# One decoder step on one core: two instruction blocks instead of four, with loads and splits moved across the seams

## The chip, the cores and the metric

The kernel runs on one core of one Trainium2 chip. The metric is the device time of one execution in microseconds (us). A core has TensorE (PE in the rows), which multiplies matrices, VectorE (DVE), ScalarE (ACT), GpSimd (POOL) and the queue engine SyncE (SP), which issues most DMAs. Each engine works through its own list of instructions in order, and they meet at semaphores.

## The reference

One step of a hybrid decoder layer, for a prompt of 1024 tokens (with 16 meta tokens ahead of it) and for 8 running sequences of 8 new tokens each, with 4096 cached positions per sequence:

```
xn = rms_norm(x, g_attn);  proj = xn @ w_in             # pool channels, q latent, kv latent, k rope, gates
q  = rms_norm(rope(rms_norm(q_lat) @ w_uq));  k = rms_norm([c_kv @ w_uk, k_rope])
prompt:  o = softmax(q k^T * SCALE, causal) @ (c_kv @ w_uv)
samples: ctx = softmax(q K^T * SCALE) @ c_all;  o = ctx @ w_uv   # c_all: the pages of the cache and the new rows
h  = x + (sigmoid(g1) * pool_mixer(u) + sigmoid(g2) * o) @ w_o
y  = h + relu(rms_norm(h) @ w_ff1)**2 @ w_ff2
```

All is float32. The products that need full precision are made of three passes over a high and a low part (`three_pass`): a number x is split into `hi`, a rounded copy (ScalarE), and `lo = x - hi` (VectorE or GpSimd).

## The kernel before, in words

The program has four stages, each in a block of its own. A block ends for all engines together: its DMAs have landed, semaphores are cleared, the engines meet at a barrier, and only then does the first instruction of the next block start.

1. `front` (to about 414 us). First the latents, queries and keys per tile of 128 tokens; then 20 chunks of 128 columns of `w_in` for the pool channels and the gates. For chunk c, SyncE loads `raw` (L242), ScalarE makes `wh` (L382), VectorE `wl` (L486), TensorE runs `project(c)` (L777) and, between the projections, the small `pooled` products (L787). ScalarE takes the sigmoid of the result (L405), VectorE scales the pooled part (L679), and GpSimd stores each pair of gate chunks to DRAM (`gated`, L282). Behind the last chunk load SyncE writes the states (L244 to L248).
2. `prompt_attention` (422 to 646 us). Its work is a list of items, each a block of values or a block of probabilities, in phases: phase -1 makes the values of the first pair of heads (9 items), and phases 0 to 15 belong to the units (head h, half qc of the queries; unit u is head u // 2). While the items of phase u run, the four score tiles of unit u + 1 are made (`score`, L104 to L106, L1167), every second item where a phase has 9 items or more, else every item. Each score tile goes through VectorE (maximum, L1135), ScalarE (`Exp`, L1084), VectorE (reciprocal) and GpSimd (scaling, L1001) before TensorE turns it (L1211) in the next phase. Phases of even u with h below 6 hold values too (9 or 10 items); phases 12 and 14 have 5 items. Queries and keys of a head are split in one phase: high by ScalarE (L1058), low by GpSimd (L984), at the items that `qk_split_at` names. For head 0 they, and the values' first weights, are loaded and split at the stage's start (L1008 to L1012, L1058, L1062, L1101, L1105).
3. `sample_attention` (649 to 1255 us). 64 groups of 4 cache pages. The last sequence is handled apart: two halves of its context (`first`, `second`: L1727, L1729) are made in banks 2 and 3, and VectorE joins them (L1783 to L1790).
4. `tail` (from 1256 us). TensorE turns the samples' contexts (L2099), multiplies them by `w_uv` (L2106), then runs the output projection `product(half, k, n)` over 8 chunks k of the mixed rows (`mh`, `ml`) and `w_o` (`woh`, `wol`); then the MLP in a loop of 16 passes over three groups of tiles. The last group holds tiles 6, 7 and 8, where tile 8 is the samples' 64 rows, of which a second half is folded in at the very end (L2212). Loads of the mixed rows (L1876), of `w_o` (L1879) and of `w_uv` (L1881) all start with the block.

Of the kernel before, what the change touches and what calls it, by code (L numbers as in the profile page):

```python
# [25 lines left out]
P = 128  # L26
# [8 lines left out]
H = 8  # L35
# [73 lines left out]
def f32(ap):  # L109
    return ap.bitcast(F32)  # L110
# [13 lines left out]
def front(nc, A, C, ps, tiles, xh, xl, cTh, cTl, Q, G, y):  # L124
# [14 lines left out]
    with ExitStack() as ctx:  # L139
        sb, sem = stage_allocator(nc, ctx)  # L140
# [44 lines left out]
        gain_in, table_in, gq_in, pages_in = sem("fr_gain_in"), sem("fr_table_in"), sem("fr_gq_in"), sem("fr_pages_in")  # L185
# [10 lines left out]
        kept = [sem(f"m_kept{i}") for i in range(2)]  # L196
        M = {k: sem("m_" + k) for k in ("wh", "wl", "proj", "up", "uc", "prevp", "prevc", "pool_d", "chain", "sig",
                                        "poolp", "gp", "tailp", "tailc", "tailo")}
        block = ctx.enter_context(nc.Block())
# [50 lines left out]

        @block.gpsimd
        def _(pool):
# [30 lines left out]
            for i in range(2):  # L283
                pool.wait_ge(kept[i], 16 * KD // 2)
# [6 lines left out]
        def _(act):  # L291
# [171 lines left out]
            for c in range(2, NCH):  # L463
                if c < 4:
                    copy_channels(c)
                else:
                    sigmoid(c)
                if c + 2 < NCH:
                    split_chunk(c + 2)

        @block.vector
        def _(dve):
# [196 lines left out]
            for j in range(KD):  # L669
                if 6 + 2 * j < NCH:  # L670
                    split_chunk(6 + 2 * j)
                for b, (lo, hi) in enumerate(groups):
                    i = 3 * j + b

                    if b == 2 and 7 + 2 * j < NCH:
# [5 lines left out]
                                                   op0=ALU.mult, op1=ALU.mult).then_inc(M["gp"], 1)  # L681

# [174 lines left out]
def prompt_attention(nc, A, C, ps, cTh, cTl, Q, G, m, B, arrived, c_rows):  # L857
# [41 lines left out]
    for u in range(-1, len(units)):  # L899
        todo = phase_items(u)  # L900
        phase_start[u] = len(items)
        apart = 2 if len(todo) >= 9 else 1
        for n, item in enumerate(todo):
            items.append(item)
            scored = u + 1 < len(units) and n % apart == 0 and n // apart < NT
            tile_at.append(NT * (u + 1) + n // apart if scored else None)
# [5 lines left out]
    qk_split_at = {phase_start[2 * h] + 1 + 2 * k: (h + 1, k) for h in range(H - 1) for k in range(2)}  # L912
    w_split_at = {phase_start[4 * (p - 1) - 1] + 7: p for p in range(1, H // 2)}
# [12 lines left out]
    with ExitStack() as ctx:  # L926
        sb, sem = stage_allocator(nc, ctx)
        w_raw = sb("pa_w_raw", [P, 2, 2 * VH])
        w_h, w_l = sb("pa_w_h", [P, 2, 2, 2 * VH], F32R), sb("pa_w_l", [P, 2, 2, 2 * VH], F32R)
        qh, ql = sb("pa_qh", [QK, 2, SEQ], F32R), sb("pa_ql", [QK, 2, SEQ], F32R)  # L930
        kh, kl = sb("pa_kh", [QK, 2, TP], F32R), sb("pa_kl", [QK, 2, TP], F32R)
        vh, vl = sb("pa_vh", [P, 2, NK, 2 * VH], F32R), sb("pa_vl", [P, 2, NK, 2 * VH], F32R)
        prob = [(sb("pa_prob0", [P, sum(wide[:NT])]), range(NT)), (sb("pa_prob1", [P, sum(wide[NT:])]), range(NT, 2 * NT))]
        raw = [sb("pa_q_raw", [QK, SEQ]), sb("pa_k_raw", [QK, TP])]
        gm, mixed = sb("pa_gm", [P, 2, 2, QC]), sb("pa_mixed", [P, 2, QC])
        ph, pl = sb("pa_ph", [P, 4, QC], F32R), sb("pa_pl", [P, 4, QC], F32R)
        late = sb("pa_late", [P, P])
        late_r, ident_r = sb("pa_late_r", [P, P], F32R), sb("pa_ident_r", [P, P], F32R)
        ntop, den, rden = sb("pa_ntop", [P, NT]), sb("pa_den", [P, NT]), sb("pa_rden", [P, NT])
        w_in, g_in, raw_in = sem("pa_w_in"), [sem(f"pa_g_in{i}") for i in range(2)], [sem("pa_q_in"), sem("pa_k_in")]  # L940
        m_out = [sem(f"pa_m_out{i}") for i in range(2)]
        S = {k: sem("pa_" + k) for k in ("late0", "late", "const", "w_hi", "w_lo", "qk_hi", "k_lo", "q_lo", "scores", "max",
                                         "exp", "rden", "scaled", "t", "hi", "lo", "pv", "out", "m")}
        block = ctx.enter_context(nc.Block())
        flat = ps[:].rearrange("p b n -> p (b n)")
        sources = ((raw[0][:], qh, ql), (raw[1][:], kh, kl))
# [33 lines left out]
        def _(pool):  # L980
            def low(h, k):
                src, hi, lo = sources[k]
                pool.wait_ge(S["qk_hi"], 2 * h + k + 1)
                nc.gpsimd.tensor_tensor(lo[:, h % 2, :], src, f32(hi[:, h % 2, :]),  # L984
                                        ALU.subtract).then_inc(S["k_lo" if k else "q_lo"], 1)

            nc.gpsimd.memset(B["c_new"][:, 0:KV], 0.0).then_inc(arrived["zeros"], 1)
            nc.gpsimd.memset(B["c_new"][:, KV:KV + 1], 1.0)
            nc.gpsimd.memset(late[:], 0.0).then_inc(S["late0"], 1)
            pool.wait_ge(S["late0"], 1)  # L990
            nc.gpsimd.affine_select(out=late[:], in_=late[:], compare_op=ALU.is_ge, fill=NEG, base=0,
                                    pattern=[[1, P]], channel_multiplier=-1).then_inc(S["late"], 1)
            low(0, 0)
            for n in range(N):
                if n in qk_split_at:
                    low(*qk_split_at[n])
# [8 lines left out]
        def _(sp):  # L1005
            def load_values(p):
                cols = A["w_uv"].rearrange("(k p) h d -> p k (h d)", p=P)[:, :, 2 * VH * p:2 * VH * (p + 1)]
                sp.dma_start(w_raw[:], cols).then_inc(w_in, 16)  # L1008

            def load_head(h):  # L1010
# [1283 lines left out]
```

## Time and profile before

| | us |
|---|---|
| median of 3 runs (lowest, highest) | 2149.71 (2149.37, 2150.7) |
| the profiled execution's own time | 2148.84 |
| its span, first to last instruction | 2146.9 |
| TensorE busy in it | 2069.8 (96%) |
| VectorE, ScalarE, GpSimd busy | 1177.6, 814.9, 384.4 |
| mean granted TensorE clock, share of full speed | 0.984 |

TensorE leaves 77.1 us of the span idle. The granted clock has two levels, full (2.4 GHz, shown as 1.00) and half (1.2 GHz, shown as 0.50). A row of the timeline reads: start in us, duration in us, engine, line, operation, output <- inputs, shape, count, and in brackets how long the engine had been idle and what released it. "SPq" is SyncE's DMA queue.

### The profile page before, as it was taken

To read this page: it belongs to the slowest core of one execution; us is meant where nothing else is said; L and a number is where in the kernel's file an instruction comes from. 1 tells how busy PE (TensorE), PEld (TensorE's weight loads), DVE (VectorE), ACT (ScalarE), POOL (GpSimd) and SP (SyncE) were. 2 spreads that over 40 slices of the span, in tenths; PEclk is the share of its full clock that TensorE was granted. 3 is DMA by queue.
4 is the path that set the end of the run, shared out by engine and by line. 5 is a ranking of instruction groups with operands and counts; after the bars stand their busy time and mean duration, and the time that the engine had idled before them with its cause. 6 is when DMAs were issued, how large, how long until landed. Compare 5 with 4: busy or idle time off the path is not lost. (4 is left out here: it accounts for less than half of the span.)

```text
span 2146.9 us, 35239 instructions
## 1 busy us (share of the span) xinstructions
PE 2069.8 (96%) x12669; PEld 1909.3 (89%) x12669; DVE 1177.6 (55%) x2356; ACT 814.9 (38%) x1589; POOL 384.4 (18%) x441
## 2 busy tenths in 40 slices
PE   7999999799988999999999989999999999999998
PEld 6889999688878999999999968889999899998997
DVE  5773311167756777767776743554444444445444
ACT  5552111166644566656665632321111122111121
POOL 2110000044421155535553510000000000000000
PEclk9999999899998999999999989999999999999999
DMA  4332222235313222222222062111111111111102
GB/s 169 92 105 71 61 82 87 92 89 165 107 50 83 57 56 67 62 73 65 66 64 73 15 213 86 46 53 41 57 39 39 39 39 59 39 54 44 39 20 89
DMA packets 146190, 152.69 MB, mean 71 GB/s; under 512 B 50694, under 2 KB 122102, under 8 KB 145021
## 3 DMA queue, kind: packets, MB, share of 16 engines
q1 hardware_dynamic: 140325, 128.28, 20.4%
q0 software_dynamic: 5728, 22.65, 3.3%
q8 instruction: 77, 1.26, 0.3%
q14 instruction: 60, 0.49, 0.1%
HBM read 124.77 MB, written 25.97 MB: 70 GB/s over the span
## 5 line engine op out<-in xcount | busy, mean ns | idle before, releaser
L104 PE MATMUL ps<-mh,f_w1h 128*128 128x384 f32 (+1 forms) x768 | 250.6, 326 | 0.0
L106 PE MATMUL ps<-mh,f_w1l 128*128 128x384 f32 (+1 forms) x768 | 250.5, 326 | 0.0
L105 PE MATMUL ps<-ml,f_w1h 128*128 128x384 f32 (+1 forms) x768 | 250.3, 326 | 0.0
L2042 ACT ACTIVATE tail_room<-ps 128x384 f32<-128x384 f32 (+1 forms) x96 | 45.5, 474 | 502.1 <-PE ps L106 502.1
L1495 ACT ACTIVATE sq<-ps 128x512 f32<-128x512 f32 x256 | 153.0, 598 | 208.9 <-PE ps L106 208.8
L2087 DVE TENSOR_TENSOR t_m<-t_m,ps 128x512 f32<-128x512 f32 x256 | 171.7, 685 | 107.0 <-PE ps L106 107.0
L105 PE MATMUL ps<-f_late_l,f_late_h 128*128 128x512 f32 x512 | 199.9, 390 | 0.0
L106 PE MATMUL ps<-f_late_h,f_late_l 128*128 128x512 f32 x512 | 199.8, 390 | 0.0
L104 PE MATMUL ps<-f_late_h 128*128 128x512 f32 x512 | 199.3, 389 | 0.0
L2067 DVE TENSOR_TENSOR tail_room<-tail_room 128x384 f32<-128x384 f32 (+1 forms) x96 | 51.5, 536 | 253.7 <-ACT tail_room L2042 253.7
L104 PE MATMUL ps<-wq,cTh 128*128 128x320 f32 x512 | 172.0, 336 | 2.3 <-DVE g_attn_b L1575 1.5
L1577 DVE TENSOR_REDUCE ss<-sq 128x8 f32<-128x512 f32 x256 | 172.9, 675 | 0.0
L106 PE MATMUL ps<-wq,cTl 128*128 128x320 f32 x512 | 158.2, 309 | 0.0
L105 PE MATMUL ps<-wq,cTh 128*128 128x320 f32 x512 | 157.8, 308 | 0.0
L104 PEld LDWEIGHTS ps<-mh,f_w1h 128*128 128x128 f32 x768 | 144.2, 188 | 1.9
L105 PEld LDWEIGHTS ps<-ml,f_w1h 128*128 128x128 f32 x768 | 144.2, 188 | 1.8
L106 PEld LDWEIGHTS ps<-mh,f_w1l 128*128 128x128 f32 x768 | 144.1, 188 | 0.0
L106 PE MATMUL ps<-w_late,cTl 128*128 128x256 f32 x512 | 143.3, 280 | 0.0
L104 PE MATMUL ps<-w_late,cTh 128*128 128x256 f32 x512 | 143.0, 279 | 0.0
L105 PE MATMUL ps<-w_late,cTh 128*128 128x256 f32 x512 | 143.0, 279 | 0.0
L1575 DVE TENSOR_TENSOR g_attn_b<-ps,g_attn_b 128x64 f32<-128x64 f32 x256 | 56.8, 222 | 151.7 <-ACT sq L1495 150.3
L106 PEld LDWEIGHTS ps<-f_late_h,f_late_l 128*128 128x128 f32 x512 | 96.1, 188 | 20.2
(348 smaller groups left out, 5029.9 us busy)
## 6 DMA issues: line engine op xcount, KB each, us to landing
f_raw<-in_w_ff SPq DMA_DIRECT2D x32, 1024.0 KB, 5.3
c_ring<-in_cache_kv_latent SPq DMA_DIRECT2D x192, 128.0 KB, 2.0
m_raw<-in_w_in SPq DMA_DIRECT2D x20, 512.0 KB, 4.0
gated<-gate POOLq DMA_DIRECT2D x8, 1088.0 KB, 4.7
pa_gm<-gated SPq DMA_DIRECT2D x16, 512.0 KB, 4.6
c_early<-in_cache_kv_latent SPq DMA_DIRECT2D x64, 128.0 KB, 2.1
fr_x<-in_x_prompt SPq DMA_DIRECT2D x8, 512.0 KB, 3.6
mixed<-pa_mixed SPq DMA_DIRECT2D x16, 256.0 KB, 2.1
```

The source lines that it names most:

```text
L104: nc.tensor.matmul(out, lh, rh, start=first, stop=False)
L105: nc.tensor.matmul(out, lh, rl, start=False, stop=False)
L106: return nc.tensor.matmul(out, ll, rh, start=False, stop=last)
L1495: nc.scalar.activation(sq[:, j % 2, :].rearrange("p (a n) -> p a n", a=2), ps[:, kn_bank(j):kn_bank(j) + 2, 0:HALF], ACT.Square).then_inc( ...
L1575: nc.vector.tensor_tensor(summed[:, p1, j * HQ:(j + 1) * HQ], ps[:, kn_bank(j), HALF:HALF + HQ], rope[:, p1, j * HQ:(j + 1) * HQ], ALU.add ...
L1577: nc.vector.tensor_reduce(ss[:, p1, j * H:(j + 1) * H], sq[:, j % 2, :].rearrange("p (h d) -> p h d", d=NOPE), AX.X, ALU.add).then_inc(S[" ...
L2042: nc.scalar.activation(z[:, a, 0:w], ps[:, 2 * par + a, 0:w], ACT.Relu).then_inc(S["relu"], 1)
L2067: nc.vector.tensor_tensor(z[:, a, 0:w], z[:, a, 0:w], z[:, a, 0:w], ALU.mult).then_inc(S["z"], 1)
L2087: nc.vector.tensor_tensor(part, part, ps[:, bank, :], ALU.add).then_inc(S["y"], 1)
```

## The change

- `front` and `prompt_attention` share one block, `sample_attention` and `tail` another. At both merged seams the engines no longer meet, and explicit waits stand for what has to be over.
- The prompt's tiles are laid out ahead of the front (`prompt_tiles`), so that those of head 0 lie on room that is free before the front ends. SyncE loads head 0's queries, keys and value weights behind the state writes, ScalarE splits them after chunk 15, VectorE and GpSimd make the low parts after step j = 5 of the last loop.
- Phase -1 starts with a value item and scores at items 1, 3, 5, 7 (before 0, 2, 4, 6). Later weights are split at item 4 of their phase, not 7. Head 7 is split in phase 11, not 12.
- SyncE issues the loads of `w_uv`, of three chunks of `w_o` and of four chunks of mixed rows while the samples end; ScalarE and VectorE split the first two or three before `second` is over. TensorE puts output products ahead of and between the turning of the contexts and their product with `w_uv`.
- In the MLP the pieces of the last group go in the order tile 8, 6, 7; the fold stands before the last addition, and the last tile's two halves are stored one by one.

```diff
@@ front, sync
             sp.wait_ge(M["tailo"], 16 * (2 + NSEQ))
+            sp.wait_ge(M["pool_d"], 8)
+            for done in qk_out:
+                sp.wait_ge(done, 16 * N)
+            load_head(nc, Q, T, E, 0)
+            load_values(nc, A, T, E, 0)
@@ front, gpsimd: for j in range(KD)
                 pool.dma_start(G[j], gate[:, j % 2]).then_inc(kept[j % 2], 16)
-            for i in range(2):
-                pool.wait_ge(kept[i], 16 * KD // 2)
+                if j == KD - 3:
...
+                    pool.wait_ge(E["qk_hi"], 1)
+                    nc.gpsimd.tensor_tensor(T["ql0"][:], T["raw_q"][:], f32(T["qh0"][:]), ALU.subtract).then_inc(E["q_lo"], 1)
@@ front, scalar: for c in range(2, NCH), after split_chunk(c + 2)
+                if c == NCH - 5:
+                    act.wait_ge(E["w_in"], 16)
+                    nc.scalar.activation(T["w_h0"][:], T["w_raw"][:], ACT.Copy).then_inc(E["w_hi"], 1)
+                    act.wait_ge(E["raw_in"][0], 16)
+                    nc.scalar.activation(T["qh0"][:], T["raw_q"][:], ACT.Copy).then_inc(E["qk_hi"], 1)
+                    act.wait_ge(E["raw_in"][1], 16)
+                    nc.scalar.activation(T["kh0"][:], T["raw_k"][:], ACT.Copy).then_inc(E["qk_hi"], 1)
@@ front, vector: for j in range(KD)
+                if j == KD - 3:
+                    dve.wait_ge(E["w_hi"], 1)
+                    nc.vector.tensor_tensor(T["w_l0"][:], T["w_raw"][:], f32(T["w_h0"][:]), ALU.subtract).then_inc(E["w_lo"], 1)
+                    dve.wait_ge(E["qk_hi"], 2)
+                    nc.vector.tensor_tensor(T["kl0"][:], T["raw_k"][:], f32(T["kh0"][:]), ALU.subtract).then_inc(E["k_lo"], 1)
@@ prompt_attention
+        first = 1 if u < 0 else 0
...
-    qk_split_at = {phase_start[2 * h] + 1 + 2 * k: (h + 1, k) for h in range(H - 1) for k in range(2)}
-    w_split_at = {phase_start[4 * (p - 1) - 1] + 7: p for p in range(1, H // 2)}
+    qk_split_at = {phase_start[2 * h] + 1 + 2 * k: (h + 1, k) for h in range(H - 2) for k in range(2)}
+    qk_split_at.update({phase_start[2 * (H - 2) - 1] + 3 + 2 * k: (H - 1, k) for k in range(2)})
+    w_split_at = {phase_start[4 * (p - 1) - 1] + 4: p for p in range(1, H // 2)}
@@ prompt_attention, tensor
+                if s == 0:
+                    pe.wait_ge(S["mask"], 2)
+                if s == 1:
+                    pe.wait_ge(E["gp"], 3 * H)
...
-            pe.wait_ge(S["const"], SEQ // P - 1 + 2)
+            pe.wait_ge(E["sig"], 2 * H)
@@ tail, sync
+            sp.wait_ge(SA["ctx"], NG - 12)
+            sp.dma_start(raw2[:], A["w_uv"].rearrange("(k p) h d -> p k (h d)", p=P)).then_inc(uv_in, 16)
+            sp.wait_ge(SA["rope"], NG)
+            for i in range(3):
+                load_o(i)
+            sp.wait_ge(SA["ctx"], NG - GS)
+            for k in range(4):
+                load_m(k)
...
@@ tail, tensor
+            pe.wait_ge(SA["gmax"], NSEQ + 1)
+            pe.wait_ge(SA["summed"], GP * NG)
+            pe.wait_ge(SA["sq"], GP * NG)
+            pe.wait_ge(SA["scaled_first"], 1)
+            head(0, (0, 1, 2, 4))
+            pe.wait_ge(SA["ctxn"], NSEQ)
             for rc in range(2):
                 for b in range(NSEQ):
                     last = nc.tensor.transpose(...)
                 last.then_inc(S["ctx_turned"], 1)
+            head(0, (3,))
+            head(1, range(5))
             pe.wait_ge(uv_in, 16)
...
+            for k in range(2):
+                head(k, (5, 6))
+            pe.wait_ge(S["gated"], 1)
+            for k in range(2):
+                head(k, (7,))
+            for k in range(2, KD):
+                head(k, range(NT - 1))
@@ tail
-    pieces = [[(t, hf) for t in g for hf in range(2)] for _c, g in groups]
+    pieces = [[(t, hf) for t in g for hf in range(2)] for g in ((0, 1, 2), (3, 4, 5), (8, 6, 7))]
@@ tail, vector: dve_step, after the addition of piece i
+                    if i == 4 and not valid(2):
+                        dve.wait_ge(folded_in, 16)
+                        dve.wait_ge(S["y"], 6 * (NS - 1) + 2)
+                        nc.vector.tensor_tensor(h8[0:TS, :], h8[0:TS, :], halves, ALU.add).then_inc(folded, 1)
```

`head(k, ns)` waits for `wol` and `ml` of chunk k and runs `product(0, k, n)` for the n named. The last stores now go: `halves` once tile 8 is added (y at 2 of the last 6), tile 6, the first half of tile 7, the samples' rows after the fold, the second half of tile 7.

## Rows read from the trace of the kernel before

**Rows 1.** Waits of TensorE, whole span: who for whom, us in total, times, longest.
```profile
PE ps L104 <- DVE pa_kl L1101: 17.0, 1, 17.0
PE ps L104 <- issue: 6.7, 1, 6.7
PE ps L2106 <- DMA f_raw<-in_w_uv: 6.6, 1, 6.6
...
PE ps L1707 <- PEq L926: 4.6, 1, 4.6
```
**Rows 2.** Windows: stretch, length, busy by engine (instructions), TensorE clock, DMA share, GB/s.
```profile
431.00:434.20 3.20, 3.20 (x15) 3.20 (x16) 1.17 (x2) 0.01 (x1) 0.00 (x0) 0.50 0.27 86
607.59:611.40 3.81, 3.81 (x17) 3.60 (x17) 1.22 (x2) 1.14 (x3) 0.69 (x1) 0.50 0.02 4
1270.70:1273.90 3.20, 3.20 (x10) 2.52 (x10) 2.85 (x4) 2.78 (x4) 0.02 (x1) 0.50 1.03 399
```
**Rows 3.** Timeline of TensorE across the first seam, to the first turned probabilities.
```profile
412.60 1.37 PE L787 MATMUL ps<-dT,wpm 128*128 128x368 f32 x4
...
431.00 0.56 PE L104 MATMUL ps<-pa_kh,pa_qh 96*128 96x264 f32 x1 [17.03 <-DVE pa_kl L1101]
...
443.67 0.66 PE L1211 MATMUL ps<-ident,pa_prob 128*128 128x128 f32 x4
```
**Rows 4.** Timeline of the other engines across the first seam, one engine after another.
```profile
413.49 1.18 DVE L679 SCALAR_TENSOR_TENSOR gate<-ps,pscale,gate 128x368 f32<-128x368 f32 x2 [11.95 <-PE ps L787]
...
428.75 2.11 DVE L1101 TENSOR_TENSOR pa_kl<-pa_k_raw,pa_kh 96x1040 fp32r<-96x1040 f32 x1 [5.07 <-ACT pa_kh L1058]
...
412.80 1.20 ACT L405 ACTIVATE gate<-ps 128x368 f32<-128x368 f32 x3 [11.94 <-PE ps L777]
...
427.38 2.38 POOL L984 TENSOR_TENSOR pa_ql<-pa_q_raw,pa_qh 96x1024 fp32r<-96x1024 f32 x1 [3.97 <-ACT pa_qh L1058]
```
**Rows 5.** DMA issues of 350 to 432 us: count, KB each, median us to landing.
```profile
pa_k_raw<-k_rows SPq DMA_DIRECT2D x1, 390.0 KB, 4.8
```
**Rows 6.** Timeline of SyncE, ScalarE and VectorE in the front's last loop.
```profile
366.61 2.67 SPq L248 DMA_DIRECT2D out_state_s<-tail  x8
...
373.98 1.20 ACT L405 ACTIVATE gate<-ps 128x368 f32<-128x368 f32 x3 [10.40 <-PE ps L777]
...
387.12 1.20 ACT L405 ACTIVATE gate<-ps 128x368 f32<-128x368 f32 x3 [10.99 <-PE ps L777]
...
376.16 1.23 DVE L486 TENSOR_TENSOR m_wl<-m_raw,m_wh 128x1024 fp32r<-128x1024 f32 x1 [0.93 <-ACT m_wh L382]
```
**Rows 7.** Timeline of GpSimd in phase 12 of the prompt's attention.
```profile
605.12 2.37 POOL L984 TENSOR_TENSOR pa_kl<-pa_k_raw,pa_kh 96x1040 fp32r<-96x1040 f32 x1 [1.48 <-ACT pa_kh L1058]
```
**Rows 8.** Timeline of TensorE: start of phase 13, start of phase 15.
```profile
607.59 0.56 PE L104 MATMUL ps<-pa_kh,pa_qh 96*128 96x264 f32 x1 [6.70 <-issue]
...
632.49 1.09 PE L1211 MATMUL ps<-ident,pa_prob 128*128 128x128 f32 x4 [2.84 <-POOL pa_prob L1001]
```
**Rows 9.** Timeline of TensorE, then ScalarE, across the seam of samples and tail.
```profile
1244.60 0.64 PE L1385 MATMUL ps<-ch,prob_hl 128*128 128x258 f32 x4
...
1253.20 0.59 PE L1729 MATMUL ps<-c_new,prob 128*64 128x257 f32 x2
1255.95 1.30 PE L2099 MATMUL ps<-ident,room 64*128 64x64 f32 x16 [2.15 <-PEq L1319]
1263.89 7.09 PE L2106 MATMUL ps<-h,f_raw 128*128 128x64 f32 x32 [6.64 <-DMA f_raw<-in_w_uv]
...
1259.51 1.06 ACT L2145 ACTIVATE mh<-t_m 128x1024 fp32r<-128x1024 f32 x1 [1.63 <-DMA t_m<-mixed]
```
**Rows 10.** Timeline of VectorE, then SyncE, at the end of the kernel.
```profile
2137.37 0.69 DVE L2087 TENSOR_TENSOR h<-h,ps 128x512 f32<-128x512 f32 x1 [0.23 <-PE ps L2015]
2141.50 1.22 DVE L2212 TENSOR_TENSOR h<-h,f_raw 64x1024 f32<-64x1024 f32 x1 [3.44 <-DMA f_raw<-h]
...
2142.74 0.54 SPq L1905 DMA_DIRECT2D out_y_s<-h  x1
```

More of the change, by code:

```diff
@@ L121, in gate_chunks, with prompt_tiles, sb, load_head @@
     return cols
-def front(nc, A, C, ps, tiles, xh, xl, cTh, cTl, Q, G, y):
+def prompt_tiles(nc):
+    T = {}
+    with ExitStack() as ctx:
+        def sb(name, shape, dt=F32):
+            T[name] = ctx.enter_context(nc.sbuf_tensor("pa_" + name, list(shape), dt))
+        NK = TP // P + 1
+        wide = [min(P * (t + 2), TP) for t in range(SEQ // P)]
+        for name in ("vh", "vl"):
+            sb(name, [P, 2, NK, 2 * VH], F32R)
+        for name, n in (("qh1", SEQ), ("ql1", SEQ), ("kh1", TP), ("kl1", TP)):
+            sb(name, [QK, n], F32R)
+        for name in ("w_h1", "w_l1"):
+            sb(name, [P, 2, 2 * VH], F32R)
+        sb("prob0", [P, sum(wide[:4])])
+        sb("prob1", [P, sum(wide[4:])])
+        sb("mixed", [P, 2, 512])
+        sb("gm", [P, 2, 2, 512])
+        sb("room", [P, 80])
+        for name, n in (("qh0", SEQ), ("ql0", SEQ), ("kh0", TP), ("kl0", TP)):
+            sb(name, [QK, n], F32R)
+        sb("raw_k", [QK, TP])
+        sb("late", [P, P])
+        for name in ("ntop", "den", "rden"):
+            sb(name, [P, 4])
+        sb("room1", [P, 68])
+        for name in ("ph", "pl"):
+            sb(name, [P, 4, 512], F32R)
+        sb("ident_r", [P, P], F32R)
+        sb("late_r", [P, P], F32R)
+        sb("raw_q", [QK, SEQ])
+        sb("w_raw", [P, 2, 2 * VH])
+        for name in ("w_h0", "w_l0"):
+            sb(name, [P, 2, 2 * VH], F32R)
+    return T
+def load_head(nc, Q, T, E, h):
+    nc.sync.dma_start(T["raw_q"][:], Q[0][:, h, TS + META:TS + TP]).then_inc(E["raw_in"][0], 16)
+    nc.sync.dma_start(T["raw_k"][:], Q[1][:, h, TS:TS + TP]).then_inc(E["raw_in"][1], 16)
+def load_values(nc, A, T, E, p):
+    cols = A["w_uv"].rearrange("(k p) h d -> p k (h d)", p=P)[:, :, 2 * VH * p:2 * VH * (p + 1)]
+    nc.sync.dma_start(T["w_raw"][:], cols).then_inc(E["w_in"], 16)
+def front(nc, A, C, ps, tiles, xh, xl, cTh, cTl, Q, G, y, block, T, E):
     N = len(tiles)
@@ L195, in front @@
         prev_in, map_in = sem("m_prev_in"), sem("m_map_in")
[L196 to L199, printed above, removed]
+        M = {k: sem("m_" + k) for k in ("wh", "wl", "proj", "uc", "prevp", "prevc", "pool_d", "chain",
+                                        "poolp", "tailp", "tailc", "tailo")}
+        M["sig"], M["gp"], kept, pages_in = E["sig"], E["gp"], E["kept"], E["pages_in"]
         w_all = A["w_in"].rearrange("(k p) n -> p k n", p=P)
@@ L926, in prompt_attention @@
     with ExitStack() as ctx:
[L927 to L940, printed above, removed]
+        _sb, sem = allocator(nc, ctx)
@@ new lines, in prompt_attention @@
+        two = lambda name: [T[name + "0"][:], T[name + "1"][:]]
+        w_h, w_l, qh, ql, kh, kl = (two(name) for name in ("w_h", "w_l", "qh", "ql", "kh", "kl"))
+        vh, vl, gm, mixed, ph, pl, late, late_r, ident_r, ntop, den, rden, w_raw = (
+            T[name] for name in ("vh", "vl", "gm", "mixed", "ph", "pl", "late", "late_r", "ident_r", "ntop", "den", "rden", "w_raw"))
+        prob = [(T["prob0"], range(NT)), (T["prob1"], range(NT, 2 * NT))]
+        w_in, raw_in = E["w_in"], E["raw_in"]
@@ L941, in prompt_attention @@
+        g_in = [sem(f"pa_g_in{i}") for i in range(2)]
         m_out = [sem(f"pa_m_out{i}") for i in range(2)]
-        S = {k: sem("pa_" + k) for k in ("late0", "late", "const", "w_hi", "w_lo", "qk_hi", "k_lo", "q_lo", "scores", "max",
-                                         "exp", "rden", "scaled", "t", "hi", "lo", "pv", "out", "m")}
-        block = ctx.enter_context(nc.Block())
+        S = {k: sem("pa_" + k) for k in ("mask", "padded", "scores", "max", "exp", "rden", "scaled", "t", "hi", "lo", "pv", "out", "m")}
@@ L1806, in _, with tail @@
             steps(pool_step)(pool)
-def tail(nc, A, C, ps, room, ctxs, m_rows, G, x_tiles, results):
+        return S
+def tail(nc, A, C, ps, room, B, m_rows, G, x_tiles, results, block, SA):
     NF = FF // FB
```

262 lines of the change are left out of this document (145 added, 117 removed).

## The prediction

> **What bounds the kernel now.** TensorE is busy 2069.8 of 2146.9 us on the page. So I read first who kept it waiting, over the whole span [rows 1]. The reader is to see that a few single waits make most of the idle time, and each has a place: 17.0 us for head 0's low part of the keys (the seam front to prompt), 6.7 us labelled "issue" inside the prompt's attention, 6.6 us for a load of `w_uv` behind the seam samples to tail, and 4.6 us at the seam prompt to samples. Then the windows around these places [rows 2]: TensorE's clock stands at 0.50 for over 3 us behind each of three gaps, so each also costs half of that stretch. Then the timelines of all engines at each place [rows 3 to 10], to see what is late next. Through the MLP loop (1300 to 2137 us) TensorE waits for nothing; the change can win only at the seams, in the prompt's phases and at the end.
>
> **First seam.** TensorE's last front product ends at 412.60 + 1.37 = 413.97; it starts again at 431.00, and the first turned probabilities stand at 443.67 [rows 3]: 29.7 us. The work between 431.00 and 443.67 takes 12.67 us, of which 3.20 at half clock [rows 2], so 12.67 - 1.6 = 11.07 at full clock. The change lets it follow at once. What is late next:
> - the last sigmoid, which frees the banks, ends at 412.80 + 1.20 = 414.0 [rows 4]: nothing to speak of;
> - the first score waits for the mask's copies, which VectorE makes behind its last scaling, at 413.49 + 1.18 = 414.67 [rows 4]. With one value item ahead of it, that is 0.25 us;
> - the chain maximum, `Exp`, reciprocal, scaling. It now starts one item later, and the weights' split stands in it at item 4. By the same durations it ends about when TensorE wants it; I take 0.3 us, bounds 0 and 3 (the whole wait of 2.84 us that phase 15 has for the same chain [rows 8]).
>
> New length about 11.07 + 0.6 = 11.7, gain 29.7 - 11.7 = 18.0 us, between 15 and 18.6.
>
> **What the moved loads and splits cost in the front.** SyncE's state writes are issued until 366.61 + 2.67 = 369.3 [rows 6]; with some 2 to 3 us until they have landed, the three loads go out at about 372, and the slowest kind lands 4.8 us after issue [rows 5]: about 377. ScalarE, which by then stands at its wait behind chunk 15, makes three high parts (some 2.7 us) until 380. Queued behind them are its sigmoid of 373.98 and the split of chunk 18, now done by about 382; VectorE waits with them, makes the two low parts, and its low part of chunk 18, which stood at 376.16, ends at about 383.5. TensorE needs it when chunk 17 is through, which ended before the sigmoid at 387.12 [rows 6]. So 3.5 us are to spare, and the splits cost nothing: project(17) hides them. GpSimd waits there too, but its next store is not due before step 6 is over. If that cover were gone, each us beyond is a us; bounds 0 and 5 us. VectorE's low part of the keys took 2.11 us beside GpSimd's low part of the queries, and ended 1.1 us after it [rows 4], as if it had done nothing before. The Trainium skill ("SBUF — State Buffer", section "Who interferes with whom") has the rule: a VectorE instruction with both inputs in SBUF is shut out while a GpSimd instruction reads SBUF. By that rule the pair takes up to 1.1 us more in its new place too, and VectorE's later subtractions can be held there; my margin shrinks to 2.4 us and stays a margin, and the sum stays as it is.
>
> **Head 7's split.** The 6.7 us are no issue time. TensorE starts at 607.59 with the first score of head 7 [rows 8], and that needs the low part of its keys, which GpSimd ended at 605.12 + 2.37 = 607.49 [rows 7]. Phase 12 has 5 items with a score at each, so two GpSimd instructions of 2.4 us do not fit between its four scalings. After the change they lie in phase 11. The gap goes (6.7), and so does the half clock behind it, 3.81 us [rows 2], worth 1.9: together 8.6. What is late next is the scaling of the last tile: phase 14 has the same shape without a split, and there TensorE waits 2.84 us for it [rows 8]. In phase 13 the first score of head 7 (1.5 us at half clock, about 1.0 at full) covers part: 1.5 to 1.8 stay. In phase 11 the two low parts push the last scaling behind the time at which phase 12 starts, by about 1 us; it has 9 items, but no values to fill it. So 8.6 - 1.7 - 1.4 = 5.5 us, between 2.5 (phase 12's gap comes back in phase 11 with a clock dip) and 7.5.
>
> **Seam prompt to samples.** It stays a block's end; its 4.6 us [rows 1] and the samples' preparation at half clock stay. 0, between -1 and 1 (more semaphores are cleared there).
>
> **Seam samples to tail.** The last product of `second` ends at 1253.20 + 0.59 = 1253.79 [rows 9]. Before: 2.15 idle, 1.30 turning the contexts, 6.64 idle, 7.09 for `w_uv` at half clock, then output products with 3.20 us at half clock [rows 2, 9], to 1273.9: 20.1 us. The same work at full clock is 1.30 + 7.09 / 2 + 1.6 = 6.45. Is all else ready? The mixed rows are loaded from the 56th context group on, which ends at 1244.60 + 0.64 = 1245.24 [rows 9]. In the old seam the first of them reached ScalarE at 1259.51 [rows 9], 3.6 us after the block's start at 1255.9; the same puts it at 1248.9, `mh` at 1250, `ml` (1.2 us) at 1251.2 and chunk 1 a little over 1 us later, at 1252.5. TensorE is then in `second` until 1253.79, so both are there. The join of the contexts (three small VectorE instructions) has four output products, about 2.8 us, beside it, ScalarE's copies have six (4 us), and `w_uv` was loaded long before. DMA is nearly idle from 1200 to 1255, so the loads collide with nothing. Gain 20.1 - 6.45 = 13.65; I take 13.6. If the first chunks came 3 us late and the clock fell, 9; at best 14.5.
>
> **The end.** TensorE ends at 2137.3; the last addition is done at 2137.37 + 0.69 = 2138.06, then `halves` lands (3.44 us idle), the fold takes 1.22, the samples' rows are stored from 2142.74 [rows 10], and the span ends 4.16 us later. After: tile 8 is added about 5 us before TensorE's end, `halves` lands before or around the fourth addition (a 1.5 MB store of tiles 3 to 5 is on the queues then), the fold goes between the fifth and sixth addition, which moves the sixth by some 0.5 to 1 us, to about 2138.8. Its store takes the same 4.16 us: 2143.0, and with the slower landing 2143.6. Gain 3.7, between 2.5 and 4.2.
>
> **Loop.** The other order of the last group changes nothing while each addition (0.69 us) is shorter than TensorE's piece. 0 us.
>
> **The sum.** 18.0 + 5.5 + 13.6 + 3.7 = 40.8 us. Against the profiled execution's 2148.84: 2108.0. The median of the runs, 2149.71, is 0.9 above that execution, so 2109 is my number.
>
> **Rivals.**
> 1. *The front pays* (head 0's loads come too late for ScalarE and VectorE, which hold back chunk 18). For it: SyncE waits until ten small writes have landed, and a 1088 KB store starts at about 376. Against: the 3.5 us of room above. 3 us of stall and a clock dip of 1.6: 2113.6.
> 2. *The tail starts hungry* (mixed rows too late, TensorE stands between `second` and the first output product, and the clock drops). For it: only 8.5 us lie between the 56th group and the end of `second`, and four 512 KB loads start together. Against: an empty queue. 4.6 us: 2113.6.
> 3. *The exponent chain or phase 11 takes back what is won* (TensorE waits for scalings in phase 0 and phase 12). For: the first scores and splits come later in their phases; against: small pieces. 3 us on each of the two terms: 2115.
> 4. *Slower than before.* With tile 8 first, TensorE's two short pieces (4 matmuls for 6) open the group's bank cycle, and VectorE still has the squares and low parts of the next group to do; if each of the 16 passes stalled TensorE, the price would be 16 times the stall. It decides from 40.8 / 16 = 2.6 us a pass; at 3 us, 48 - 40.8 = 7 us slower: 2157. Against: TensorE has no wait in that loop, and VectorE is busy only half of it.
> 5. *It does not do what it says*: if the engines still met at the merged seams (a wait that stands for a barrier, say that of the front's last GpSimd store), only head 7 and the end would win: 2149.7 - 9.2 = 2140.5.
>
> **How the numbers follow.** Forecast 0.74, rivals 1 and 2 0.08 each, 3 0.05, 4 0.03, 5 0.01, others of no effect 0.01. The likeliest gives 2109. All terms at their best are 44.8 + 1 = 45.8, thus 2104; rivals 1 to 3 reach 2115, and two of them together 2119. Range 2104 to 2119. This kernel's measurement tells about 0.2% from no change (4.3 us); faster by more: 0.96, within: 0.01, slower: 0.03.
>
> **What would show it.** Right: at the first seam TensorE's wait for `pa_kl` is gone and its clock stays 1.00 from 410 to 430; no wait at chunk 18; in phase 13 a wait under 2 us for GpSimd instead of 6.7; output products directly behind `second` at full clock; about 5.5 us from TensorE's last product to the end, for 9.55 now; the seam prompt to samples as before. Wrong: a wait of TensorE for `m_wl` near 387, a gap before the first output product, a wait over 3 us at the start of phase 12, or TensorE idle in the MLP loop.

## The result, and the profile after

| | before | after |
|---|---|---|
| median of 4 runs (lowest, highest), us | 2149.64 (2149.37, 2150.7) | 2117.85 (2117.62, 2120.17) |
| ratio, 95% interval | | 0.9855 (0.9843 to 0.9867) |
| the profiled execution's own time, span | 2148.84, 2146.9 | 2120.17, 2118.4 |
| TensorE busy, granted clock | 2069.8, 0.984 | 2072.5, 0.994 |

The gain is 31.8 us, inside the range of the forecast and 9 short of its 40.8. The profiled execution of after is the slowest of its four, so between the two traces the gain is 28.5 us. To see where it lies, I read the same events of TensorE in both timelines; the last column is one of the experiments further down, put beside them here because it answers the question that the first two raise.

| time from the start of the span to, us | before | after | won by then | aligned version, won by then |
|---|---|---|---|---|
| first turned probabilities | 443.67 | 427.42 | 16.25 | 16.90 |
| end of the prompt's attention | 644.42 | 622.38 | 22.04 | 23.11 |
| start of the samples | 649.00 | 627.54 | 21.46 | 22.53 |
| end of `second` | 1253.79 | 1232.29 | 21.50 | 24.07 |
| first product of `w_ff1` | 1377.50 | 1344.35 | 33.15 | 37.55 |
| last product | 2137.34 | 2111.49 | 25.85 | 37.35 |
| end of the span | 2146.9 | 2118.4 | 28.5 | 39.5 |

The line to stop at is the last product: between 1344 and 2111 us, where the forecast had put 0, after gives back 7.3 us. Everything before it went nearly as forecast. First the waits of TensorE in after (who for whom, us in total, times, longest), which answer to [rows 1]:

```profile
PE ps L785 <- DVE fr_xn L604: 8.9, 1, 8.9
PE ps L1284 <- POOL pa_prob L1077: 7.2, 5, 2.9
PE ps L1779 <- PEq L2383: 5.2, 1, 5.2
...
PE ps L104 <- DVE pa_vl L1212: 0.5, 1, 0.5
```

The 17.0, the "issue" of 6.7 and the 6.6 for `w_uv` are gone; the seam prompt to samples stays, at 5.2 us where it was 4.6. None of the waits in the list lies in the MLP. The timeline of TensorE in after at the first seam, in phase 13 and across the seam of samples and tail (start, duration, engine, line, operation), answering to [rows 3, 8, 9]:

```profile
413.46 1.37 PE L868 MATMUL ps<-dT,wpm 128*128 128x368 f32 x4
414.92 0.39 PE L104 MATMUL ps<-pa_w_h,p_cTh 128*128 128x256 f32 x1
...
427.42 0.66 PE L1284 MATMUL ps<-ident,pa_prob 128*128 128x128 f32 x4
...
588.14 0.63 PE L1284 MATMUL ps<-ident,pa_prob 128*128 128x128 f32 x4 [1.89 <-POOL pa_prob L1077]
...
1231.70 0.59 PE L1801 MATMUL ps<-c_new,prob 128*64 128x257 f32 x2
1232.23 0.50 PE L104 MATMUL ps<-f_w1h,mh 128*128 128x512 f32 x1
...
1235.21 1.21 PE L2223 MATMUL ps<-ident,room 64*128 64x64 f32 x16
...
1240.61 3.68 PE L2232 MATMUL ps<-h,f_raw 128*128 128x64 f32 x32
```

The reader is to see three things: the first value product at 414.92 follows the front's last product, which ends at 414.83, with no gap worth the name; the 6.70 us ahead of head 7's score have become 1.89 for a scaling; and the output products follow `second` with no bracket at all, the product with `w_uv` at 3.68 us in place of 7.09. The clock at the two seams (windows of after: stretch, length, busy by engine with the instructions in brackets, TensorE clock, DMA share, GB/s), where [rows 2] had 0.50:

```profile
414.90:430.00 15.10, 14.40 (x101) 12.95 (x101) 10.08 (x31) 8.73 (x23) 2.72 (x5) 1.00 0.33 110
...
1231.70:1236.00 4.30, 4.30 (x27) 3.10 (x26) 2.81 (x6) 0.66 (x2) 1.06 (x2) 1.00 1.14 339
```

Then the front's last loop in after (SyncE's queue, ScalarE, VectorE, GpSimd), answering to [rows 6]. The moved splits are the rows of `pa_`; the "SPq" row is the first of the moved loads. The low part of chunk 18 is `m_wl`, done at 385.1, and the sigmoid behind which TensorE wants it is that of 387.98:

```profile
373.07 0.32 SPq L167 DMA_DIRECT2D pa_raw_q<-q_rows  x1
...
378.81 0.63 ACT L541 ACTIVATE pa_w_h<-pa_w_raw 128x512 fp32r<-128x512 f32 x1 [14.38 <-DMA pa_w_raw<-in_w_uv]
...
380.48 2.43 POOL L352 TENSOR_TENSOR pa_ql<-pa_raw_q,pa_qh 96x1024 fp32r<-96x1024 f32 x1 [2.67 <-ACT pa_qh L543]
381.26 1.17 ACT L473 ACTIVATE gate<-ps 128x368 f32<-128x368 f32 x3
381.38 2.62 DVE L762 TENSOR_TENSOR pa_kl<-pa_raw_k,pa_kh 96x1040 fp32r<-96x1040 f32 x1 [1.22 <-ACT pa_kh L545]
...
383.93 1.21 DVE L562 TENSOR_TENSOR m_wl<-m_raw,m_wh 128x1024 fp32r<-128x1024 f32 x1
...
387.98 1.20 ACT L473 ACTIVATE gate<-ps 128x368 f32<-128x368 f32 x3 [4.60 <-PE ps L858]
```

And the end in after (VectorE and SyncE's queue), answering to [rows 10]: the fold comes first, and the last addition stands behind it.

```profile
2111.45 1.22 DVE L2195 TENSOR_TENSOR h<-h,f_raw 64x1024 f32<-64x1024 f32 x1 [0.64 <-DMA f_raw<-h]
2112.60 0.67 DVE L2191 TENSOR_TENSOR t_m<-t_m,ps 128x512 f32<-128x512 f32 x1
...
2113.30 0.57 SPq L2009 DMA_DIRECT2D out_y_p<-t_m  x1
```

**The 7.3 us of the MLP.** TensorE is never idle there, and runs the same products. So I grouped its products between 1400 and 2090 us, each shape by itself (line, engine, operation, names, shape, count, busy us, mean ns of one, idle us before). Before:

```profile
L106 PE MATMUL ps<-f_late_h,f_late_l 128*128 128x512 f32 x466 | 181.8, 390 | 0.0
L105 PE MATMUL ps<-f_late_l,f_late_h 128*128 128x512 f32 x465 | 181.6, 390 | 0.0
L104 PE MATMUL ps<-f_late_h 128*128 128x512 f32 x465 | 181.0, 389 | 0.0
L104 PE MATMUL ps<-mh,f_w1h 128*128 128x384 f32 x463 | 155.0, 335 | 0.0
...
L106 PE MATMUL ps<-mh,f_w1l 128*128 128x384 f32 x462 | 154.7, 335 | 0.0
```

After:

```profile
L105 PE MATMUL ps<-f_late_l,f_late_h 128*128 128x512 f32 x463 | 183.5, 396 | 0.0
L106 PE MATMUL ps<-f_late_h,f_late_l 128*128 128x512 f32 x463 | 181.8, 393 | 0.0
L104 PE MATMUL ps<-f_late_h 128*128 128x512 f32 x462 | 181.6, 393 | 0.0
L106 PE MATMUL ps<-mh,f_w1l 128*128 128x384 f32 x464 | 156.9, 338 | 0.0
L104 PE MATMUL ps<-mh,f_w1h 128*128 128x384 f32 x464 | 155.8, 336 | 0.0
```

The products of 512 columns (the second matrix, in the tiles `f_late_h` and `f_late_l`) take 3 to 6 ns more. From start to start it is 227.9 ns before and 231.9 after, over the three kinds; with 36 of them in a full group that is 8.19 us before and 8.35 after, and over a pass 0.42 us, 16 passes 6.7 us. Small, but on an engine that is busy without a break there is nothing that hides it. The first matrix (tiles `f_w1h` and `f_w1l`) shows little: its products of 384 columns take 334 or 335 ns before and 335 to 338 after. From start to start the products of the first matrix add up to 371.9 us over the MLP before and 372.4 after, those of the second to 368.5 and 375.0.

Two things differ there: the order of the pieces, which the prediction had weighed, and the places of the tail's tiles. The merged block lets the tail's first tiles fill while the samples still use theirs, so `mh`, `ml`, `f_late_h`, `f_late_l` and h were given other places, and the eighth part of `f_late_l` became a tile of its own. Before, the tail's tiles all start 416 bytes over a multiple of 2048 in their partition; after, `f_late_l` starts at 928 and `f_late_h` at 1536. The traces hold no addresses: such places are added up from the tiles' sizes in the kernels.

### The profile page after: what moved, and what is told of

It is laid out like the page before. It is cut to its first block, busy times and chain, and to the rows that moved or that the text cites. A ratio compares the mean times of both kernels' runs of the same rounds, so it can differ in the third digit from the quotient of the medians.

```text
span 2118.4 us, 35220 instructions
## 1 busy us (share of the span) xinstructions
PE 2072.5 (98%) x12669; PEld 1903.3 (90%) x12669; DVE 1174.0 (55%) x2356; ACT 814.3 (38%) x1589; POOL 384.6 (18%) x441
## 4 chain that ended last, share of the span: by engine, by line
PE 66%; DVE 2%; ACT 1%; issue 1%; DMA 0%; DVEq 0%
PE ps L104 19%; PE ps L106 19%; PE ps L105 19%; PE ps L1498 2%; PE ps L1457 1%; PE ps L1463 1%; PE ps L2118 1%; DVE ss L1649 0%; DVE cTl L1655 0%; ACT sq L1567 0%; PE ps L2072 0%; PE ps L2116 0%; PE ps L2119 0%; DVE var L1725 0%; PE ps L1555 0%
## 5 line engine op out<-in xcount | busy, mean ns | idle before, releaser
L104 PE MATMUL ps<-mh,f_w1h 128*128 128x384 f32 (+1 forms) x768 | 251.0, 327 | 0.0
L104 PE MATMUL ps<-f_late_h 128*128 128x512 f32 x512 | 201.2, 393 | 0.0
L104 PE MATMUL ps<-wq,cTh 128*128 128x320 f32 x512 | 172.0, 336 | 2.4 <-DVE g_attn_b L1647 1.8
L104 PEld LDWEIGHTS ps<-mh,f_w1h 128*128 128x128 f32 x768 | 144.2, 188 | 2.1
L104 PE MATMUL ps<-w_late,cTh 128*128 128x256 f32 x512 | 143.0, 279 | 0.0
L104 PEld LDWEIGHTS ps<-f_late_h 128*128 128x128 f32 x512 | 96.3, 188 | 22.2
```

What stands on the lines that cost most here:

```text
L104: nc.tensor.matmul(out, lh, rh, start=first, stop=False)
```

## Experiments

### The two merged seams, each alone

`s1_first_merge` has the front and the prompt's attention of after, samples and tail of before; `s2_second_merge` the reverse.

> Front and prompt's attention as after (one block, early loads of head 0, head 7 split in phase 11), samples and tail as before. Theory (the terms of the profile of after add up and do not touch each other): the first turned probabilities 17 us earlier counted from the front's end, phases 11 to 13 another 5.8, nothing else: 23 us, so 2127. Rival (the slower pace of the 512-column products in the MLP comes with the block structure): part of it shows here too, products at over 0.230 us and a gain of 16 to 20. Forecast's own terms: 18.0 + 5.5 = 23.5.

> Front and prompt's attention as before, samples and tail as after (one block, other layout of the tail's tiles, last group in the order 8, 6, 7, early fold). Theory: the seam itself gives 13.6, the end 2.7, and the MLP loop gives back 7 us, because its 512-column products take 0.2320 instead of 0.2277 us: 8 to 9 us net, 2141. Rival (the slower pace was a matter of that one execution): products at 0.2277 and 15 to 17 us net, 2133.

Measured: 2127.22 us (ratio 0.9896, 0.988 to 0.9913) and 2141.71 us (0.9963, 0.9948 to 0.9977). The first merge wins 22.8 us of 2149.98, the second 8.3; together 31.1, and both at once 31.8. So as far as these intervals tell (some 3 us either way) they do not help or hinder each other. What each still waits for at seams, from TensorE's waits (for whom, us in total, times, longest). First merge alone:

```profile
PE ps L2179 <- DMA f_raw<-in_w_uv: 6.3, 1, 6.3
...
PE ps L2172 <- PEq L1392: 2.1, 1, 2.1
```

Second merge alone:

```profile
PE ps L104 <- DVE pa_kl L1101: 16.8, 1, 16.8
...
PE ps L104 <- issue: 6.7, 1, 6.7
```

Each loses exactly the waits of its own seam. The MLP, from its first product to its last, takes 759.84 us in the first and 767.14 in the second: the slow products come with the second merge.

### Order of the pieces, or places of the tiles

`o1_order_only` is the kernel before with one line of after, `l1_layout_only` the kernel before with the tail's places of after:

```diff
 o1:
-    pieces = [[(t, hf) for t in g for hf in range(2)] for _c, g in groups]
+    pieces = [[(t, hf) for t in g for hf in range(2)] for g in ((0, 1, 2), (3, 4, 5), (8, 6, 7))]
 l1:
-        mh = sb("mh", [P, KD, TOK], F32R)
-        ml = sb("ml", [P, KD, TOK], F32R)
...
+        _room0 = sb("t_room0", [P, 128])
+        mh = sb("mh", [P, KD, TOK], F32R)
+        late_l = sb("f_late_l", [P, (KD - 1) * 512], F32R)
...
+        m = sb("t_m", [P, H, SEQ])
         late_h = sb("f_late_h", [P, KD * 512], F32R)
-        late_l = sb("f_late_l", [P, KD * 512], F32R)
```

> The kernel before with one edit: the last group's pieces in the order tile 8, 6, 7. Theory A (address): no change of pace, 2149 to 2150, at most 0.5 us at the very end, since the samples' rows are added earlier but stored as before. Theory B (order): 36 products take 8.35 us instead of 8.19 and the time goes up by 6 to 7 us, 2156.

> The kernel before with one edit: the tail's tiles lie at the addresses that they have in the kernel after. Theory A (where the operands lie in SBUF sets the pace of the 512-column products): each takes 0.2315 to 0.2325 us instead of 0.2277 in the MLP, 36 products 8.35 us instead of 8.19, the time goes up by 6 to 9 us, to 2156 to 2159. Theory B (the order of the last group sets it): no change, 2149 to 2150.

Measured: 2149.96 us for the order (1.0001, 0.9992 to 1.0011; MLP 760.04) and 2158.48 us for the places (1.0041, 1.0027 to 1.0055; MLP 767.06). The order is free, as forecast. The places alone, with not one instruction changed, cost 8.5 us (9.5 between the spans): 7.2 in the MLP and some 1.8 in the output projection in front of it. That projection takes 109.35 us from its first product to the MLP's, for 106.76 before, but 4.7 us of it stand at half clock here and 3.2 before, which makes 0.8 of the 2.6. With the clock full throughout, after takes 112.12 us for the same work and the aligned version 110.31: again 1.8.

### Which property of a place

The first five are before or after with nothing but padding tiles put in ([P, 8] is 8 numbers, 32 bytes, per partition); the last gives after's tail another order of tiles. Padding behind a pair keeps the tiles after it where they were. In `p2` this puts `f_late_l` 1856 over a multiple of 2048, not 1024 as its expectation says; the distance is the one it names.

```diff
 p1 (before):  +        _pad0 = sb("t_pad0", [P, 128])     # ahead of late_h; 384 more behind late_l
 p2 (before):  +        _pad0 = sb("t_pad0", [P, 360])     # between late_h and late_l; 152 behind
 d5 (before):  +        _pad0 = sb("t_pad0", [P, 128])     # between late_h and late_l; 384 behind
 d2 (before):  +        _pad = sb("t_pad", [P, 8])         # ahead of all tiles of the tail
 a2 (after):   +        _room1b = sb("t_room1b", [P, 8])   # ahead of ml; room2 8 less
               +        _room3 = sb("t_room3", [P, 8])     # ahead of late_h
 a1 (after):
-        _room0 = sb("t_room0", [P, 128])
+        late_l7 = sb("f_late_l7", [P, 512], F32R)
         mh = sb("mh", [P, KD, TOK], F32R)
         late_l = sb("f_late_l", [P, (KD - 1) * 512], F32R)
...
-        _room2 = sb("t_room2", [P, 608])
+        late_h7 = sb("f_late_h7", [P, 512], F32R)
+        st = sb("f_st", [P, NT, 4])
+        _room2 = sb("t_room2", [P, 244])
...
-        late_h = sb("f_late_h", [P, KD * 512], F32R)
+        _room3 = sb("t_room3", [P, 232])
+        late_h = sb("f_late_h", [P, (KD - 1) * 512], F32R)
```

> The kernel before with 512 bytes of padding ahead of f_late_h and 1536 behind f_late_l: both tiles start 512 bytes further (928 over a multiple of 2048, where everything in the tail stood at 416), their distance from one another stays 0 over a multiple of 2048, and all other tiles stand at 416 as before. Theory A (where a tile starts by itself sets the pace of the products that read it): the 36 products of a second-matrix group go from 8.19 us to about 8.35 and the time from 2150 to 2156 or so. Theory B (what counts is how the two tiles that one product reads lie to each other): late_h and late_l still lie alike, 8.19 us and 2150.

> The kernel before with 1440 bytes of padding between f_late_h and f_late_l (608 behind them): late_l starts 1024 over a multiple of 2048, late_h stays at 416, so their distance over a multiple of 2048 is the one of the kernel after. Theory B (the distance between the two tiles of one product): products that read both, 105 and 106, slow down by some 5 ns each, those of line 104 (late_h alone) do not; a group of 36 takes about 8.3 us and the time is 2153 to 2156. Theory A (each tile's own start): only the products with late_l as moving operand change, if 1024 is a bad place; 2150 to 2153. If neither, 2150.

> The kernel before with 32 bytes of padding ahead of all of the tail's tiles, so that each starts on a multiple of 64, 448 over a multiple of 2048, and their distances stay what they were. Theory B (the distance over 64 between the tiles counts, not the place): as before, 8.19 us a group and 2150. Theory C (a tile on a multiple of 64 is a slow one, one at 32 over is fast): all 512-column products slow down, L104 as well, 8.35 us or more and 2156 to 2161.

> The kernel after with three paddings only: ml (with h8, m8 and f_late_l7 behind it) starts 32 bytes later and so do f_late_h and f_raw2. So all operands of the tail's products start 32 over a multiple of 64, as in the kernel before; over a multiple of 2048 they stand at 416, 928, 1184 and 1568, so not alike. Theory (the runs so far fit it: 512-column products are slow where late_h and late_l lie 32 bytes apart over a multiple of 64, in after, in the layout put into before, in the tiles 1440 bytes apart, and in the version meant to be aligned, where late_h stood at 448 for a rounding; fast where they lie alike): the group of 36 products takes 8.19 to 8.22 us instead of 8.35 and the time is 2109.5 to 2112. Rival (places have to be alike over 2048 bytes or more, or 64 plays no part): 8.33 us or more, 2116 to 2119.

> The kernel before with 512 bytes of padding between f_late_h and f_late_l (1536 behind them): they lie 512 apart over a multiple of 2048, late_h at 416 and late_l at 928. Distances of 32, 608 and 640 over a multiple of 2048 gave 764.7 to 767.1 us for the MLP, 0 gave 759.8 to 760.0. If the pace repeats every 512 bytes (or 256): 759.8 to 760.3 and 2150. If it wants 1024 or the whole 2048 of one operand's row: 764.5 to 766 and 2155 to 2157.

> The kernel after with its tail's tiles moved so that each starts 416 over a multiple of 2048, as in the kernel before (f_late_h and f_late_l keep their first seven parts and have the eighth apart; h also stays in its place, 320 over). If the places of f_late_h, f_late_l, mh and ml are all that slowed the 512-column products, a group of 36 products goes from 8.35 us back to 8.19 and the time from 2117.9 to about 2109.5 to 2111.5. Rival (the pace came from something else that the merged block has, such as another place of h): 2116 to 2118, groups stay at 8.35.

| kernel | late_h against late_l, bytes over a multiple of 2048 (of 512) | second matrix, mean ns from start to start | MLP on TensorE, us | median, us |
|---|---|---|---|---|
| before | 0 (0) | 227.9 | 759.84 | 2149.6 to 2150.2 |
| both tiles 512 further (`p1`) | 0 (0) | 227.9 | 759.84 | 2150.01 |
| all tiles 32 further (`d2`) | 0 (0) | 227.9 | 759.85 | 2149.86 |
| 512 apart (`d5`) | 1536 (0) | 227.9 | 759.84 | 2149.62 |
| 1440 apart (`p2`) | 608 (96) | 231.9 | 765.88 | 2156.97 |
| places of after in before (`l1`) | 608 (96) | 231.8 | 767.06 | 2158.48 |
| after | 608 (96) | 231.9 | 767.14 | 2117.85 |
| after, 32 bytes put in twice (`a2`) | 640 (128) | 231.1 | 764.74 | 2115.9 |
| after, meant to be aligned (`a1`) | 32 (32) | 231.7 | 765.75 | 2117.94 |

Shifting both tiles by 512 bytes, or all by 32, leaves the MLP's time to the hundredth of a us. Changing their distance to 608 makes it longer: `p2`, which changes nothing else of what the MLP reads, has the whole slowdown of the second matrix (368.5 to 374.9 us over the MLP, 375.0 in after). Nor is it the place of one of them: the slow `a1` has `f_late_h` at 448, where it stands in the fast `d2`, and `f_late_l` at 416, where it stands before. The clearest pair is the one with padding between the two tiles, in the groups of 1400 to 2090 us. Padding of 1440 bytes:

```profile
L105 PE MATMUL ps<-f_late_l,f_late_h 128*128 128x512 f32 x469 | 185.9, 396 | 0.0
L104 PE MATMUL ps<-f_late_h 128*128 128x512 f32 x468 | 184.0, 393 | 0.0
L106 PE MATMUL ps<-f_late_h,f_late_l 128*128 128x512 f32 x468 | 183.9, 393 | 0.0
```

Padding of 512 bytes:

```profile
L106 PE MATMUL ps<-f_late_h,f_late_l 128*128 128x512 f32 x467 | 182.3, 390 | 0.0
L105 PE MATMUL ps<-f_late_l,f_late_h 128*128 128x512 f32 x466 | 182.0, 391 | 0.0
L104 PE MATMUL ps<-f_late_h 128*128 128x512 f32 x466 | 181.4, 389 | 0.0
```

My theories fell one by one here. "Each tile's own start" fell with `p1` and `p2`, and the forecast that L104, which reads `f_late_h` alone, stays as it is fell with `p2` (393 ns). "Alike over a multiple of 64" fitted all kernels run by then and was not enough: after with 32 bytes put in has its operands alike over 64 and regains 2.4 us of 7.3 (2115.9, ratio 0.9842, 0.9829 to 0.9856). Of the 2.4 the second matrix, whose products read `f_late_h` and `f_late_l` alone, has 1.3, and keeps 5.2 of its 6.5; the first matrix has most of the rest. That places alike over 64 but not over 512 keep most of the loss rests on this one kernel, which also has `ml` elsewhere than the others. And the first aligned version missed (2117.94 for 2109.5 to 2111.5) for a plain reason: the allocator starts a tile on a multiple of 32 bytes, `f_st` (144 bytes) and the padding behind it (976) are not such multiples, each was rounded up by 16, and `f_late_h` stood at 448, not 416.

### The aligned version

```diff
 against the version that was meant to be aligned:
-        _room3 = sb("t_room3", [P, 232])
+        _room3 = sb("t_room3", [P, 224])
```

> The kernel after with its tail laid out so that w1h, w1l, mh, ml, f_late_h and f_late_l all start 416 over a multiple of 2048 (h stays where it was, at 1568): the version meant to be aligned before, less the 32 bytes that stood in it. Theory D (late_h and late_l must lie a multiple of 2048, or of a power of two between 64 and 2048, apart: 0 gave 759.84 us for the MLP on TensorE in four kernels; 32, 608 and 640 gave 765.8, 765.9 to 767.1, and 764.7): the MLP takes 759.8 to 760.5 us instead of 767.1 and the time is 2109 to 2111. Rival (the distance must be a multiple of 4096 or more, here it is 45 times 2048, or the slowness has to do with h or with the input's raw tiles, which this kernel has in other places): 764 us or more, 2114 to 2118.

Measured: 2109.82 us (2109.2 to 2110.92), ratio to before 0.9815 (0.9801 to 0.9828) where after has 0.9855 (0.9843 to 0.9867), 8.0 us less than after; the MLP takes 760.04 us. It differs from the version that was meant to be aligned by 32 bytes in the place of `f_late_h` and of the raw tile behind it, and by 8.1 us. Of the 9.4 us between the two traces, 6.4 lie where the tiles are read (MLP 765.75 to 760.04, output projection 111.02 to 110.31) and 1.65 in the samples, which go with the clock (end of the next part); the rest lies in the front and the prompt's attention, which are the same in both. It is faster than before and than after. Its groups of 1400 to 2090 us:

```profile
L105 PE MATMUL ps<-f_late_l,f_late_h 128*128 128x512 f32 x468 | 182.6, 390 | 0.0
L104 PE MATMUL ps<-f_late_h 128*128 128x512 f32 x469 | 182.6, 389 | 0.0
L106 PE MATMUL ps<-f_late_h,f_late_l 128*128 128x512 f32 x468 | 182.5, 390 | 0.0
```

### Head 7's split put back

```diff
-    qk_split_at = {phase_start[2 * h] + 1 + 2 * k: (h + 1, k) for h in range(H - 2) for k in range(2)}
-    qk_split_at.update({phase_start[2 * (H - 2) - 1] + 3 + 2 * k: (H - 1, k) for k in range(2)})
+    qk_split_at = {phase_start[2 * h] + 1 + 2 * k: (h + 1, k) for h in range(H - 1) for k in range(2)}
```

> The kernel after with head 7's queries and keys split in phase 12 again (the old position), all else as it is. Theory (the 5.8 us that the phases of the prompt's attention gained are the wait for that split): the wait of TensorE there is back and the time is 2117.9 + 5.8 = about 2123.7, with all of it between the start of phase 12 and the end of the prompt's attention. Rival (the gain came from the other moved pieces, the split of the last values and the late masks): at most 2119.

Measured: 2126.42 us (0.9889, 0.9872 to 0.9905), 8.6 slower than after. The theory holds: the rival had 2119 at most. Its size holds less well. The wait is back, in TensorE's timeline:

```profile
591.56 0.56 PE L104 MATMUL ps<-pa_kh,pa_qh 96*128 96x264 f32 x1 [6.74 <-issue]
```

and the prompt's attention ends at 628.60 instead of 622.38, 6.2 us later; the last product comes 6.4 later. That is what the trace shows of the 8.6. The rest is the 2.3 us by which the profiled execution of after lies above its median: against profile and profile the difference is 2126.55 - 2120.17 = 6.4.

## Why the prediction was right, and by how much it missed

| term | forecast | after | aligned version |
|---|---|---|---|
| first seam, to the first turned probabilities | 18.0 | 16.25 | 16.90 |
| head 7's split and the phases | 5.5 | 5.8 | 6.2 |
| seam prompt to samples | 0 | -0.6 | -0.6 |
| samples | 0 | 0 | 1.5 |
| seam samples to tail, to the MLP | 13.6 | 11.65 | 13.5 |
| MLP | 0 | -7.3 | -0.2 |
| the end | 3.7 | 2.65 | 2.15 |
| sum (between the traces) | 40.8 | 28.5 | 39.5 |

- **The step that failed is the loop's.** The sum had 0 us for it; it gave back 7.3. "The other order of the last group changes nothing" was right (`o1_order_only`: 1.0001). "0 us" for the loop was wrong, because I priced only what the diff does to the order of instructions there and not that it moves the tiles the products read (`l1_layout_only`: 767.06 us for 759.84 with the order of before). It also ate most of what the seam samples to tail lacks: 13.5 in the aligned version against 11.65. That is 7.1 + 1.85 = 9 us of the 12.3 that are missing between the traces.
- **First seam.** The mechanism was as told: no wait for `pa_kl`, clock at 1.00, first scores after the masks, one short wait of 0.46 us for a low part of the values. From the front's last product it is 29.70 before, 12.59 after: 17.1 won. The 12.59 are 0.9 more than my 11.7; the short wait is half of that, the rest is not traced. And the front's own end came 0.86 later, which varies between executions (413.96 to 414.90 in the eight with before's front, 414.04 to 416.07 in the six with after's).
- **The moved splits in the front.** Hidden, as forecast. The loads went out at 373.07 for 372, the low part of the keys took 2.62 us where it had taken 2.11, and 2.8 us were to spare of the 3.5 (`m_wl` done at 385.14, the sigmoid at 387.98). In both places it ended 1.1 us after GpSimd's low part of the queries: at 384.00 behind 382.91 now, at 430.86 behind 429.76 before [rows 4]. The 0.5 us more are the 0.5 us by which it now starts nearer to GpSimd's start (0.90 behind it, for 1.37). The Trainium skill's "SBUF — State Buffer", section "Who interferes with whom", says that a VectorE instruction with two inputs in SBUF contends with a GpSimd instruction that reads SBUF, and that the one that comes second is blocked until the first is done; both rows agree with it.
- **Head 7.** 6.70 became 1.89 (forecast 1.5 to 1.8), and no gap opened in phase 12. The 1.4 us that I took off for phase 11 is not to be seen there as a gap. That the clock stays at 1.00 behind the 1.89 is luck in part: the same wait stands in `s1_first_merge` (1.91) and `a2_after_32_bytes` (1.90), and there the clock fell to 0.50 at 588.22 and 588.90, for 3.4 and 6.8 us, and the phases won 4.6 and 4.4 us for 5.8.
- **The seam samples to tail.** All of it was ready, as the sum had it: no bracket from 1231.70 to 1244, 3.68 us for `w_uv`, clock 1.00.
- **The end.** 1 us short; 6.9 us from TensorE's last product to the end. I had said 5.5, which does not go with my own sum: 9.55 less the 3.7 is 5.85. `halves` landed only behind the fifth addition (the fold waited 0.64 us for it), the fold held the sixth until 2112.60 where TensorE ended at 2111.49, and the last store took longer to the span's end (5.1 us from its issue at 2113.30, where I took 4.16 from the samples' store).
- **The rivals.** None took place. The slower one decided from 2.6 us a pass; the pass did get slower, by 0.42, but from the tiles' distance and not from tile 8. So the place of 2117.85 inside the range is luck in part: the room up to 2119 was there for rivals 1 to 3, and a loss that I had not thought of used it.

The samples take 604.8 us in some executions and 603.3 in others, whichever block and whichever places they have (604.8 in before and after, 604.9 with head 7 put back; 603.3 in both single merges, in `l1_layout_only` and in the aligned version). The clock tells them apart. Behind the seam prompt to samples it falls for the last time ahead of the tail for 13.65 us in all seven traces of the first kind and for 10.24 us in all seven of the second (3.4 us less at half clock are worth 1.7). The windows, in before and in the aligned version:

```profile
656.11:669.76 13.65, 11.35 (x52) 10.83 (x51) 5.83 (x11) 3.92 (x8) 0.76 (x2) 0.50 0.34 81
...
634.55:644.79 10.24, 7.94 (x37) 7.42 (x36) 4.21 (x8) 3.32 (x7) 0.76 (x2) 0.50 0.37 87
```

Why it is the one or the other in an execution is open. It is 1.5 us of a trace's error, and the reason that the aligned version's column wins there.

## What to carry to other kernels

When stages are merged so that one's first work runs under the other's last, the gain can be summed from the gaps, with the half-clock stretch behind each of them, and here it came true to some 2 us a term. But such a merge also moves tiles: list where every operand of the busiest engine starts before and after, and keep the operands of one product at the distances they had. Here that was worth 8.0 us, a quarter of what the merge itself won. An engine that is never idle shows such a loss only in the mean length of one instruction, so compare that too, by shape, and not the waits alone.

## What the runs showed of the hardware that was not expected

- The pace of three-pass products of 512 columns depends on the distance in bytes between the tiles they read. 0 and 1536 over a multiple of 2048 gave 759.8 to 760.0 us for the MLP's 4000 or so products of both matrices; 32, 608 and 640 gave 764.7 to 767.1. These fit a pace that repeats at 512 bytes; 1024 was not tried, nor 256 (128, which 640 is over 512, was not enough in the one kernel that has it). The mean of one product goes from 390 to 393 and 396 ns.
- A product whose operands lie in one tile (L104 of the second matrix, high by high) slows down too, from 389 to 393. What it shares with its neighbours, and so the mechanism, no run here tells. That the weights of one product are loaded while the one before it streams would fit (weight loads are busy 1909.3 us and products 2069.8 of the same 2146.9), and is only argued.
- The products of 384 columns hardly show it: 334 ns each with `f_late_h` and `f_late_l` 608 apart (`p2`), 334 or 335 before. In after, where `mh` and `ml` have other places as well, they take 335 to 338.
